# Which work stands ahead of what at the start, in the last gate groups and at the last store of a Strassen-multiplied decoder layer

## The chip, the cores and the metric

The kernel runs on one core of a Trainium2 chip. The metric is the device time of one execution in microseconds (us), as the median over several runs; lower is better. The profile is one further execution of the same program, recorded by the hardware profiler; it has a time of its own, which stands beside its span below. The core's engines are TensorE (PE in the rows, its weight loads PEld), VectorE (DVE), ScalarE (ACT), GpSimd (POOL) and SyncE (SP), which here only issues transfers.

## The reference

A decoder layer over 512 rows of width 2048 in float32. One projection makes seven blocks of 2048 columns and 16 forget logits; a causal depthwise convolution of 31 taps feeds one half of the output projection, an attention with forget gates the other; a layer norm ends it.

```python
z = einsum("bsd,de->bse", h, w_in) + b_in
glu_val, glu_gate, gate_c, q, k, v, f_logit, gate_a = split(z)
u = glu_val * sigmoid(glu_gate)
c = depthwise_causal_conv(u, w_dw, taps=31) + b_dw
y_conv = silu(layer_norm(c)) * silu(gate_c)
logits = q k^T * scale + cum[:, :, q0:q1, None] - cum[:, :, None, :q1]   # cum = cumsum(log_sigmoid(f_logit))
y_attn = softmax(causal(logits)) v * silu(gate_a)
h = layer_norm(ALPHA * h + concat(y_conv, y_attn) w_out + b_out)
```

## The kernel before

**Products.** Every float32 operand is split into a rounded part (a copy on ScalarE into fp32r, `high`, `x_high`, L797, L804) and what is left of it (a subtraction on VectorE, `low`, `x_low`, L1325, L1371). A product is three matmuls: high by high, high by low, low by high (`mm3`, L1073 to L1075). The projections follow Strassen's scheme with seven products in place of eight: x and the weights are cut into quarters, and sums of quarters of x (`X_ORDER`, factors 0 to 6) are multiplied by sums of weight blocks (`B11`, `B12`, `B22`, `SUM`, `B21`).

**Groups and slots.** There are 56 groups `g` of two weight tiles. Groups 0 to 47 (three per head: query and key, value and attention gate, convolution value and its gate) make the heads; groups 48 to 55 make the convolution's gates. `HEAD_GROUPS` is 48. A group has seven slots `s`; in a slot TensorE runs one unit of 24 matmuls (`unit(n)`), and ScalarE and VectorE make the weights of the unit two slots later (`high(n + 2)`, `low(n + 2)`). Slot 2 of a group runs the unit with m = 4 of the group before. Each engine's program is one list in a written order; an instruction that waits for a semaphore holds all behind it on its engine, and TensorE, too, takes its instructions in order.

**Sums of weight blocks.** In a group VectorE makes two sums (`sum_1`, L1336; `sum_2`, L1344), and GpSimd two with accumulating transfers (`sum_3`, L658; `sum_4`, L665). The latter gives the weights of the m = 4 unit. From group 51 on (`T4_VEC`) VectorE makes it itself (L1351).

**The start.** TensorE turns x's quarters with transposes (`turn_x`, L1139), ScalarE and VectorE round them. The forget logits have weights of their own (`f_raw`, `f_w`), rounded and multiplied beside the rest (`f_terms`, L1149 and L1151). GpSimd adds a causal mask to the rows of forget sums that SyncE has repeated over the partitions (`load_bias`, L505; `masks`, L673).

**The convolution.** A head's 31 taps are multiply-adds on VectorE (`conv`, L1432), dealt out over slots by the tables `TAPS_AT` and, for the last head, `TAPS_LAST` (a row for each group from 48 on, a number for each slot); half of a slot's taps stand ahead of its `low`, half behind. GpSimd sums the heads' results (`add_conv`, L681); when all 16 are in, one matmul with `mean_w` makes the mean (L1254), ScalarE reads it (L985), and the heads' rows are loaded back (`load_cin`, L437), centred on VectorE (`center`, L1561), squared on ScalarE (L948) and added up (`add_square`, L1568), all at the (group - 48, slot) places of `LOAD_AT`, `CENTER_AT`, `SQUARE_AT` and `ADD_AT`.

**The end.** After the groups come 112 units of the output projection and a norm. SyncE stores the rows of the output (`store_half`, L629; L635; L639).

## Time and profile before

| what | us |
|---|---|
| median of 3 runs (lowest, highest) | 1584.41 (1583.24, 1584.81) |
| the profiled execution's own time | 1583.03 |
| its span | 1581.2 |
| TensorE busy | 1552.0 (98%) |
| VectorE busy | 1445.3 (91%) |
| ScalarE busy | 840.8 (53%) |
| GpSimd busy | 248.9 (16%) |

The span runs from the first to the last instruction. A row of the timeline is: start, length, engine, line, operation, output<-input, shape, count, and in brackets how long the engine had been idle before it and what released it. Line numbers in the rows are those of the kernel before. `PEclk` is the granted TensorE clock as a share of full speed.

### The profile page before, as it was taken

Reading aid. Unit: us, or ns where it says so; the run is one execution under the profiler, and the core shown is the slowest. Engines: PE = TensorE matmul, PEld = TensorE weight load, DVE = VectorE, ACT = ScalarE, POOL = GpSimd, SP = SyncE. Lnnn points to the kernel's source line nnn. Section 1 sums busy time; section 2 is a strip of 40 time slices with the busy share of each in tenths; the row PEclk is TensorE's granted clock in tenths of the full one; section 3 lists DMA queues with packets and bytes.
Section 4 is the critical chain, followed back from the end, with each engine's and each line's share of the span. In section 5 each row is a group of like instructions: output and inputs, shape, how many; then the busy total and the mean of one; then the engine's idle time right before and its main releaser. Section 6 shows DMA issues by size and latency. Waiting matters only on the chain.

```text
span 1581.2 us, 29452 instructions
## 1 busy us (share of the span) xinstructions
PE 1552.0 (98%) x11574; PEld 1487.7 (94%) x11574; DVE 1445.3 (91%) x1975; ACT 840.8 (53%) x1225; POOL 248.9 (16%) x275
## 2 busy tenths in 40 slices
PE   7999999999999999999999999999999999999997
PEld 6999999999999999999999999999999988888885
DVE  7769999999999999999999999999989889986787
ACT  4565454554545545455454554545455576654462
POOL 1101112122121221212212122121110000000000
PEclk9999999999999999999999999999999999999998
DMA  8488889999999999999999999999899899887776
GB/s 225 113 198 190 220 203 223 220 222 233 231 228 222 222 240 224 226 219 223 236 219 233 225 221 239 224 226 218 192 275 284 238 340 343 295 238 239 267 214 192
DMA packets 316473, 365.23 MB, mean 231 GB/s; under 512 B 14561, under 2 KB 254337, under 8 KB 315025
## 3 DMA queue, kind: packets, MB, share of 16 engines
q1 hardware_dynamic: 285168, 260.45, 53.3%
q0 software_dynamic: 26784, 98.58, 34.6%
q10 hardware_dynamic: 4384, 4.33, 0.8%
q8 instruction: 92, 1.51, 0.4%
q14 instruction: 45, 0.37, 0.1%
HBM read 287.25 MB, written 87.06 MB: 237 GB/s over the span
## 4 chain that ended last, share of the span: by engine, by line
PE 85%; DVE 8%; issue 3%; DMA 2%; ACT 1%; SPq 0%; POOL 0%; DVEq 0%; ACTq 0%; POOLq 0%
PE ps L1073 28%; PE ps L1074 28%; PE ps L1075 28%; DVE whl L1325 2%; DVE c_tiles L1432 2%; PE ps L1190 1%; DVE raw L1344 1%; DMA f_raw<-in_w_in_dram 1%; DMA conv_rows_dram<-c_tiles 1%; DMA raw<-in_w_out_dram 1%; DVE xl L1371 0%; ACT whl L797 0%; PE ps L1184 0%; DVE raw L1336 0%; DMA raw<-raw 0%
## 5 line engine op out<-in xcount | busy, mean ns | idle before, releaser
L1073 PE MATMUL ps<-xh,whl 128*128 128x256 f32 x3136 | 896.1, 286 | 8.3 <-DVE whl L1325 3.7
L1074 PE MATMUL ps<-xl,whl 128*128 128x256 f32 x3136 | 888.8, 283 | 0.0
L1075 PE MATMUL ps<-xh,whl 128*128 128x256 f32 x3136 | 888.8, 283 | 0.0
L797 ACT ACTIVATE whl<-raw 128x1024 fp32r<-128x1024 f32 x392 | 415.2, 1061 | 557.9 <-PE ps L1075 472.0
L1073 PEld LDWEIGHTS ps<-xh,whl 128*128 128x128 f32 x3136 | 600.4, 191 | 11.2 <-issue 6.3
L1074 PEld LDWEIGHTS ps<-xl,whl 128*128 128x128 f32 x3136 | 600.6, 192 | 0.5 <-issue 0.5
L1075 PEld LDWEIGHTS ps<-xh,whl 128*128 128x128 f32 x3136 | 600.4, 191 | 0.0
L1325 DVE TENSOR_TENSOR whl<-raw,whl 128x1024 fp32r<-128x1024 f32 x392 | 478.7, 1221 | 56.6 <-ACT whl L797 56.5
L1432 DVE SCALAR_TENSOR_TENSOR c_tiles<-ps,taps,c_tiles 128x511 f32<-128x511 f32 (+14 forms) x480 | 350.1, 729 | 6.8
L658 POOL DMA_DIRECT2D raw<-raw x56 | 49.7, 888 | 556.4 <-DMA raw<-in_w_in_dram 446.5
L1073 PE MATMUL ps<-whl,yh 128*128 128x512 f32 x320 | 124.9, 390 | 1.2 <-issue 0.9
L1328 DVE TENSOR_TENSOR whl<-raw,whl 128x1024 fp32r<-128x1024 f32 x80 | 97.8, 1222 | 30.0 <-ACT whl L773 29.8
L1074 PE MATMUL ps<-whl,yh 128*128 128x512 f32 x320 | 124.7, 390 | 0.0
L1075 PE MATMUL ps<-whl,yl 128*128 128x512 f32 x320 | 124.6, 389 | 0.0
L773 ACT ACTIVATE whl<-raw 128x1024 fp32r<-128x1024 f32 x80 | 84.6, 1057 | 74.2 <-PE ps L1075 72.6
L665 POOL DMA_DIRECT2D raw<-raw x51 | 43.2, 848 | 310.5 <-DVE whl L1325 310.5
L1344 DVE TENSOR_TENSOR raw<-raw 128x1024 f32<-128x1024 f32 x56 | 72.7, 1299 | 1.9
L1073 PEld LDWEIGHTS ps<-whl,yh 128*128 128x128 f32 x320 | 60.1, 188 | 14.5 <-DVE whl_more L1328 1.7
L1075 PEld LDWEIGHTS ps<-whl,yl 128*128 128x128 f32 x320 | 60.1, 188 | 12.5
L1074 PEld LDWEIGHTS ps<-whl,yh 128*128 128x128 f32 x320 | 60.1, 188 | 12.4
L690 POOL DMA_DIRECT2D out_sums_dram<-in_w_out_dram x64 | 68.6, 1199 | 1.0 <-DMA out_sums_dram<-out_sums_dram 0.5
L1336 DVE TENSOR_TENSOR raw<-raw 128x1024 f32<-128x1024 f32 x56 | 68.2, 1218 | 0.0
(197 smaller groups left out, 1538.0 us busy)
## 6 DMA issues: line engine op xcount, KB each, us to landing
raw<-in_w_in_dram SPq DMA_DIRECT2D x224, 512.0 KB, 8.0
raw<-raw POOLq DMA_DIRECT2D x107, 512.0 KB, 6.0
out_sums_dram<-in_w_out_dram POOLq DMA_DIRECT2D x64, 512.0 KB, 9.6
raw<-out_sums_dram SPq DMA_DIRECT2D x64, 512.0 KB, 5.2
raw<-in_w_out_dram SPq DMA_DIRECT2D x48, 512.0 KB, 5.6
out_sums_dram<-in_w_out_dram SPq DMA_DIRECT2D x32, 512.0 KB, 9.5
out_sums_dram<-out_sums_dram SPq DMA_DIRECT2D x32, 512.0 KB, 9.4
x<-in_x_dram SPq DMA_DIRECT2D x8, 512.0 KB, 8.2
```

The costliest lines, as they stand in the source:

```text
L658: nc.gpsimd.dma_start(raw[:, ring(g, B12), :], raw[:, ring(g, B22), :], accum_op=ALU.add) \
L690: nc.gpsimd.dma_start(t_dram[t, k, :, :], src, accum_op=ALU.add).then_inc(t_added[t], 16)
L773: nc.scalar.activation(out_w(u, 0), raw_out(u), ACT.Copy).then_inc(high_done, 1)
L797: nc.scalar.activation(w_high(n), source(n), ACT.Copy).then_inc(high_done, 1)
L1073: nc.tensor.matmul(o, ah, bh, start=start, stop=False, skip_group_check=True)
L1074: nc.tensor.matmul(o, ah, bl, start=False, stop=False, skip_group_check=True)
L1075: return nc.tensor.matmul(o, al, bh, start=False, stop=True, skip_group_check=True)
L1325: vec.tensor_tensor(w_low(n), source(n), w_high(n), ALU.subtract).then_inc(low_done, 1)
L1328: vec.tensor_tensor(out_w(u, 1), raw_out(u), out_w(u, 0), ALU.subtract).then_inc(low_done, 1)
L1336: vec.tensor_tensor(raw[:, ring(g, SUM), :], raw[:, ring(g, B11), :], raw[:, ring(g, B12), :], ALU.add).then_inc(t1_done, 1)
L1344: vec.tensor_tensor(o, o, raw[:, ring(g, B22), :], ALU.add).then_inc(t2_done, 1)
L1432: vec.scalar_tensor_tensor(out=o[:, n:], in0=ps[:, U_BANK, 0:SEQ - n], scalar=tap, in1=o[:, n:], op0=ALU.mult, op1=ALU.add) \
```

## The change

The last head's taps, which stood in groups 48 to 50, stand in groups 48 to 51: group 49 has 12 in place of 15, group 50 has 10 in place of 9, and group 51 has 2. The mean matmul moves from slot 5 of group 50 to slot 2 of group 51, ScalarE's read of it from slot 6 to slot 3 of group 51, and GpSimd's addition of head 15 from group 50 to group 51. The rows of head 15 are stored by SyncE in the loads of group 52, and SyncE no longer waits for that store ahead of its other loads; the wait stands at the load of head 15 and at ScalarE's second square. Loading, centring, squaring and adding move by up to a few slots.

At the start, x's second quarter (factor 1) and the first weights are rounded ahead of the forget weights on ScalarE and VectorE, and TensorE's first unit stands ahead of the first forget terms. GpSimd's first masks stand behind `sum_4` of group 1. At the end, the first half of the first 128 output rows is stored from ScalarE's queue in place of SyncE's last place.

On ScalarE at the start, where `f_raw` and `f_w` are the forget weights, `xh` the rounded x and `whl` the rounded weights, there stood:

```order
L804 ACTIVATE xh<-ps 128x512 x4
L813 ACTIVATE f_w<-f_raw 128x16x16
L816 ACTIVATE f_w<-f_sum 128x8x16
L819 ACTIVATE f_w<-f_w 128x384
L804 ACTIVATE xh<-ps 128x512 x4
L797 ACTIVATE whl<-raw 128x1024 x2
L804 ACTIVATE xh<-ps 128x512 x4
L797 ACTIVATE whl<-raw 128x1024
```

Now there stands (the lines are those of the changed kernel):

```order
L808 ACTIVATE xh<-ps 128x512 x8
L801 ACTIVATE whl<-raw 128x1024
L819 ACTIVATE f_w<-f_raw 128x16x16
L822 ACTIVATE f_w<-f_sum 128x8x16
L801 ACTIVATE whl<-raw 128x1024
L826 ACTIVATE f_w<-f_w 128x384
L808 ACTIVATE xh<-ps 128x512 x4
L801 ACTIVATE whl<-raw 128x1024
```

The four pieces of x's second quarter and the first weights moved up past the three forget activations, and the second weights past the last of these.

On GpSimd behind the first group, where `raw` is a weight block and `probs` holds the forget sums, there stood:

```order
L658 DMA raw<-raw 128x1024
L715 TENSOR_TENSOR x<-x 128x2048
L665 DMA raw<-raw 128x1024
L658 DMA raw<-raw 128x1024
L673 TENSOR_TENSOR probs<-probs,mask 128x128 x4
L665 DMA raw<-raw 128x1024
```

Now there stands:

```order
L660 DMA raw<-raw 128x1024
L717 TENSOR_TENSOR x<-x 128x2048
L667 DMA raw<-raw 128x1024
L660 DMA raw<-raw 128x1024
L667 DMA raw<-raw 128x1024
L675 TENSOR_TENSOR probs<-probs,mask 128x128 x4
```

The masks moved behind the transfer that makes the m = 4 weights of group 1 (L665 before, L667 now); nothing else moved there.

On VectorE in slots 5 and 6 of group 49, from `sum_1` to the next weights and an eviction, where the `c_tiles` rows are taps and `th_z` is a gate, there stood:

```order
L1336 TENSOR_TENSOR raw<-raw 128x1024
L1432 SCALAR_TENSOR_TENSOR c_tiles<-ps,taps,c_tiles 128x495
L1432 SCALAR_TENSOR_TENSOR c_tiles<-ps,taps,c_tiles 128x494
L1553 SCALAR_TENSOR_TENSOR tiles<-th_z,tiles 128x512
L1432 SCALAR_TENSOR_TENSOR c_tiles<-ps,taps,c_tiles 128x493
L1325 TENSOR_TENSOR whl<-raw,whl 128x1024
L1469 TENSOR_TENSOR tiles<-nu,ps 128x256
```

Now there stands:

```order
L1345 TENSOR_TENSOR raw<-raw 128x1024
L1441 SCALAR_TENSOR_TENSOR c_tiles<-ps,taps,c_tiles 128x497
L1562 SCALAR_TENSOR_TENSOR tiles<-th_z,tiles 128x512
L1441 SCALAR_TENSOR_TENSOR c_tiles<-ps,taps,c_tiles 128x496
L1334 TENSOR_TENSOR whl<-raw,whl 128x1024
L1478 TENSOR_TENSOR tiles<-nu,ps 128x256
```

A tap's shape counts down by one column with each tap. The last tap ahead of the weights has 493 columns before and 496 now: three taps fewer have run by there, one of them in this piece and two ahead of it.

The diff, with the tables' later lines left out:

```diff
@@ -52,20 +52,20 @@
 CIN = 6
 
 
-LOAD_AT = {(3, 1): (0, 1, 2), (4, 0): (3, 4), (4, 1): (5, 6), (5, 0): (7,), (5, 1): (8, 9), (6, 0): (10, 11),
+LOAD_AT = {(3, 1): (0, 1, 2), (4, 0): (3, 4), (4, 1): (5,), (5, 0): (6,), (5, 1): (7, 8), (6, 0): (9, 10),
...
-CENTER_AT = {(3, 0): 0, (3, 3): 1, (3, 6): 2, (4, 0): 3, (4, 2): 4, (4, 3): 5, (4, 6): 6, (5, 0): 7, (5, 2): 8, (5, 3): 9,
+CENTER_AT = {(3, 4): 0, (3, 6): 1, (4, 0): 2, (4, 2): 3, (4, 3): 4, (4, 6): 5, (5, 0): 6, (5, 2): 7, (5, 3): 8, (5, 6): 9,
...
 R1, R1_ODD, R2, R5, U_BANK, BANK_A, BANK_B, BANK_C = range(8)
 
 PAIRS = ((Q, K), (V, GATE_A), (VAL, GLU))
 
 TAPS_AT = ((2, 0, 1, 2, 1, 0, 2), (2, 1, 1, 2, 3, 1, 2), (0, 1, 2, 3, 2, 1, 2))
-TAPS_LAST = ((0, 0, 0, 0, 2, 2, 3), (2, 1, 2, 2, 2, 3, 3), (2, 2, 3, 2, 0, 0, 0))
+TAPS_LAST = ((0, 0, 0, 0, 2, 2, 3), (2, 1, 1, 2, 2, 1, 3), (2, 1, 1, 2, 1, 1, 2), (2, 0, 0, 0, 0, 0, 0))
 
 PT_N = [SEQ - P * j for j in range(NT)]
 PT_AT = [0, 512, 1024, 896]
@@ -434,6 +434,8 @@
                     sp.wait_ge(cent_stored[j % CIN], 16 * (j // CIN))
                 elif j == CIN - 1:
                     sp.wait_ge(mean_var_done, 1)
+                if j == HEADS - 1:
+                    sp.wait_ge(c_stored[1], 8 * HEADS)
                 sp.dma_start(cin_slot(j), conv_dram[j, :, :]).then_inc(cin_loaded[j % CIN], 16)
 
             def loads(g):
@@ -454,6 +456,9 @@
                     sp.wait_ge(cum_stored, 16)
                     load_bias(0)
                 if g >= 1:
+                    if g == HEAD_GROUPS + 4:
+                        sp.wait_ge(conv_done, HEADS)
+                        sp.dma_start(conv_dram[HEADS - 1, :, :], c_tiles[:, 1, :]).then_inc(c_stored[1], 16)
                     for j in LOAD_AT.get((g - HEAD_GROUPS, 0), ()):
                         load_cin(j)
                     sp.wait_ge(low_done, at(g - 1, 3) + 1)
@@ -553,10 +558,8 @@
                 if g - 2 >= HEAD_GROUPS:
                     store_z2(g - 2)
                 if g == HEAD_GROUPS + 3:
-                    sp.wait_ge(conv_done, HEADS)
-                    sp.dma_start(conv_dram[HEADS - 1, :, :], c_tiles[:, 1, :]).then_inc(c_stored[1], 16)
                     sp.wait_ge(c_stored[0], 8 * HEADS)
-                    sp.wait_ge(c_stored[1], 8 * HEADS)
+                    sp.wait_ge(c_stored[1], 8 * HEADS - 16)
                     sp.wait_ge(pv_done, HEADS)
                 for j in LOAD_AT.get((g - HEAD_GROUPS, 1), ()):
                     load_cin(j)
@@ -624,7 +627,7 @@
                     if u == NORM_AT[j - 4] + 12:
                         load_z(j)
             def store_half(e, h):
-                t, c = (2, 3, 0)[e], slice(1024 * h, 1024 * (h + 1))
+                t, c = 2 + e, slice(1024 * h, 1024 * (h + 1))
                 sp.wait_ge(bpost_added, 16 * (2 * e + h + 1))
                 sp.dma_start(out[0, P * t:P * (t + 1), c], res[t][:, c]).then_inc(stored, 16)
 
@@ -637,7 +640,6 @@
                 c = slice(SEQ * n, SEQ * (n + 1))
                 sp.wait_ge(row_done, n + 2)
                 sp.dma_start(out[0, P:2 * P, c], res[1][:, c]).then_inc(stored, 16)
-            store_half(2, 0)
             sp.wait_ge(stored, 160)
 
         @block.gpsimd
@@ -713,16 +715,18 @@
                     pool.wait_ge(s3_s1_s2_done, 3)
                     pool.wait_ge(low_done, 3)
                     nc.gpsimd.tensor_tensor(x12[:, :, :], x12[:, :, :], x21[:, :, :], ALU.add).then_inc(s4_done, 1)
-                if g < HEAD_GROUPS and g % 3 == 1:
+                if 1 < g < HEAD_GROUPS and g % 3 == 1:
                     masks(g // 3)
                 if g < T4_VEC:
                     sum_4(g)
+                if g == 1:
+                    masks(0)
                 out_sums(g)
                 if g < HEAD_GROUPS and g % 3 == 0 and g >= 6:
                     add_conv(g // 3 - 2)
                 if g == HEAD_GROUPS:
                     add_conv(HEADS - 2)
-                if g == HEAD_GROUPS + 2:
+                if g == HEAD_GROUPS + 3:
                     add_conv(HEADS - 1)
 
             def repeat_row(dst, src, loaded, accum=False):
@@ -809,17 +813,17 @@
                     src = w_in[1024 * h:1024 * (h + 1), F_COL:F_COL + HEADS]
                     nc.scalar.dma_start(f_raw[:, h, :, :], src.rearrange("(k p) c -> p k c", p=P)).then_inc(f_loaded, 16)
             x_high(0)
+            x_high(1)
+            high(0)
             act.wait_ge(f_loaded, 32)
             nc.scalar.activation(f_w[:, 0:2, :, 0:HEADS].rearrange("p a k c -> p (a k) c"),
                                  f_raw[:, :, :, :].rearrange("p a k c -> p (a k) c"), ACT.Copy).then_inc(fw_high, 1)
             act.wait_ge(fw_vec, 1)
             nc.scalar.activation(f_w[:, 2, :, 0:HEADS], f_sum[:, :, :], ACT.Copy).then_inc(fw_high, 1)
+            high(1)
             act.wait_ge(fw_vec, 3)
             act.wait_ge(vec_const, 3)
             nc.scalar.activation(f_w[:, 3, :, :], f_w[:, 2, :, :], ACT.Copy, scale=-1.0).then_inc(fw_high, 1)
-            x_high(1)
-            high(0)
-            high(1)
             x_high(3)
             high(2)
             act.wait_ge(rows_turned, 1)
@@ -944,6 +948,8 @@
                 if j >= 3:
                     act.wait_ge(sq_added, j - 2)
                 nc.scalar.dma_start(conv_dram[j, :, :], cin_slot(j)).then_inc(cent_stored[j % CIN], 16)
+                if j == 1:
+                    act.wait_ge(c_stored[1], 8 * HEADS)
                 o = c_tiles[:, j % 2, :] if j else sq_sum[:, :]
                 nc.scalar.activation(o, cin_slot(j), ACT.Square).then_inc(sq_done, 1)
 
@@ -980,7 +986,7 @@
                                              ACT.Copy, scale=0.5).then_inc(taps_done, 1)
                         x_high(2)
                         forget(1)
-                    if g == HEAD_GROUPS + 2 and s == 6:
+                    if g == HEAD_GROUPS + 3 and s == 3:
                         act.wait_ge(mean_var_done, 1)
                         nc.scalar.activation(mean[:, :], ps[:, BANK_B, :], ACT.Copy).then_inc(mean_read, 1)
                     if (g - HEAD_GROUPS, s) in SQUARE_AT:
@@ -1065,6 +1071,8 @@
             deviation(2)
             scale_rows(2)
             deviation(3)
+            act.wait_ge(bpost_added, 80)
+            nc.scalar.dma_start(out[0, 0:P, 0:1024], res[0][:, 0:1024]).then_inc(stored, 16)
 
         @block.tensor
         def _(pe):
@@ -1157,9 +1165,9 @@
             for f in (0, 1):
                 for b in range(4):
                     turn_x(f, b)
-            pe.wait_ge(fw_high, 3)
+            unit(0)
+            pe.wait_ge(fw_vec, 3)
             f_terms(((0, 0, 0), (2, 0, 1)), True)
-            unit(0)
 
             def scores(i):
 
@@ -1228,6 +1236,7 @@
                     if g == 0 and s == 3:
                         f_terms(((1, 3, 1),))
                     if g == 0 and s == 5:
+                        pe.wait_ge(fw_high, 3)
                         f_terms(((3, 5, 1),)).then_inc(f_done, 1)
                         for b in range(3):
                             turn_x(2, b)
@@ -1248,7 +1257,7 @@
                         turn_p_c(g // 3 - 1)
                     if 0 < g <= HEAD_GROUPS and g % 3 == 0 and s == 4:
                         values(g // 3 - 1)
-                    if g == HEAD_GROUPS + 2 and s == 5:
+                    if g == HEAD_GROUPS + 3 and s == 2:
                         pe.wait_ge(csum_done, HEADS)
                         pe.wait_ge(ptl_done, 3 * HEADS)
                         nc.tensor.matmul(ps[:, BANK_B, :], mean_w[:, :], csum[:, :], start=True, stop=True) \
@@ -1371,8 +1380,10 @@
                         vec.tensor_tensor(lo, ps[:, x_bank(at_f + b), :], hi, ALU.subtract).then_inc(xl_done, 1)
 
             x_low(0)
+            x_low(1)
             dve.wait_ge(f_loaded, 32)
             vec.tensor_tensor(f_sum[:, :, :], f_raw[:, 0, :, :], f_raw[:, 1, :, :], ALU.add).then_inc(fw_vec, 1)
+            low(0)
             dve.wait_ge(fw_high, 2)
             dve.wait_ge(fw_vec, 1)
             vec.tensor_tensor(f_w[:, 0:2, :, LOW_AT:F_WIDE].rearrange("p a k c -> p (a k) c"),
@@ -1380,8 +1391,6 @@
                               f_w[:, 0:2, :, 0:HEADS].rearrange("p a k c -> p (a k) c"), ALU.subtract).then_inc(fw_vec, 1)
             vec.tensor_tensor(f_w[:, 2, :, LOW_AT:F_WIDE], f_sum[:, :, :], f_w[:, 2, :, 0:HEADS], ALU.subtract) \
                .then_inc(fw_vec, 1)
-            x_low(1)
-            low(0)
             for h in range(2):
                 dve.wait_ge(x_loaded["21"][h], 16)
             dve.wait_ge(xt_turned, 4)
@@ -1443,7 +1452,7 @@
                 i = g // 3 - (2 if g % 3 == 0 and s < 4 else 1)
                 if i < HEADS - 1:
                     return i, TAPS_AT[g % 3][s]
-                if g < HEAD_GROUPS + 3:
+                if g < HEAD_GROUPS + 4:
                     return HEADS - 1, TAPS_LAST[g - HEAD_GROUPS][s]
                 return 0, 0
```

## Rows read from the trace of the kernel before

**Rows 1.** TensorE's waits over the whole span: total us, times, longest.
```profile
PE ps L1073 <- DVE whl L1325: 3.7, 7, 1.5
PE ps L1073 <- DVE tiles L1473: 3.2, 3, 2.3
```

**Rows 2.** TensorE in the timeline, start.
```profile
10.45 1.09 PE L1139 MATMUL ps<-ident,x 128*128 128x128 f32 x8 [0.28 <-DMA x<-in_x_dram]
...
12.98 0.32 PE L1149 MATMUL ps<-xh,f_w 128*48 128x256 f32 x1 [1.44 <-ACT f_w L819]
...
17.13 0.38 PE L1073 MATMUL ps<-xh,whl 128*128 128x256 f32 x1 [0.20 <-DVE whl L1325]
...
20.47 0.39 PE L1073 MATMUL ps<-xh,whl 128*128 128x256 f32 x1 [0.21 <-DVE whl L1325]
...
23.45 1.91 PE L1139 MATMUL ps<-ident,xs 128*128 128x128 f32 x16
```

**Rows 3.** The load of the first weights (L427): issue, and time from issue to landing.
```profile
2.99 0.52 SPq L427 DMA_DIRECT2D raw<-in_w_in_dram  x1
...
DMA to landing us min/median/max: 9.2/9.2/9.2
```

**Rows 4.** ScalarE and VectorE in the timeline, start.
```profile
12.83 2.04 ACT L804 ACTIVATE xh<-ps 128x512 fp32r<-128x512 f32 x4
14.74 1.08 ACT L797 ACTIVATE whl<-raw 128x1024 fp32r<-128x1024 f32 x1
...
15.85 1.23 DVE L1325 TENSOR_TENSOR whl<-raw,whl 128x1024 fp32r<-128x1024 f32 x1
```

**Rows 5.** TensorE in the timeline, at its longest wait after the start.
```profile
84.58 0.58 PE L1073 MATMUL ps<-xh,whl 128*128 128x256 f32 x1 [2.26 <-DVE tiles L1473]
```

**Rows 6.** One stretch: length, busy (instructions) of PE, PEld, DVE, ACT, POOL, PEclk, DMA, GB/s.
```profile
84.50:87.90 3.40, 3.33 (x16) 3.33 (x17) 3.33 (x16) 2.50 (x7) 0.00 (x0) 0.54 0.80 218
```

**Rows 7.** VectorE and GpSimd in the timeline ahead of that wait.
```profile
64.48 1.15 DVE L1325 TENSOR_TENSOR whl<-raw,whl 128x1024 fp32r<-128x1024 f32 x1
...
75.64 1.70 POOL L673 TENSOR_TENSOR probs<-probs,mask 128x128 f32<-128x128 f32 x4 [26.62 <-DMA probs<-forget_sums_dram]
77.30 0.83 POOL L665 DMA_DIRECT2D raw<-raw  x1
```

**Rows 8.** That L665 transfer, from issue to landing.
```profile
DMA to landing us min/median/max: 4.6/4.6/4.6
```

**Rows 9.** Columns as Rows 6; a stretch, and the sum over 1100 to 1180.
```profile
1160.00:1180.00 20.00, 19.27 (x159) 18.92 (x159) 14.85 (x18) 11.11 (x16) 1.68 (x2) 1.00 1.05 313
sum 80.00, PE 75.79 PEld 73.70 DVE 73.18 ACT 36.47 POOL 12.99; mean PE 18.95 PEld 18.43 DVE 18.30 ACT 9.12 POOL 3.25
```

**Rows 10.** The page's group of the taps: busy us, mean ns, idle before.
```profile
L1432 DVE SCALAR_TENSOR_TENSOR c_tiles<-ps,taps,c_tiles 128x511 f32<-128x511 f32 (+14 forms) x480 | 350.1, 729 | 6.8
```

**Rows 11.** TensorE in the timeline, the two longest idles of groups 49 and 50.
```profile
1135.93 0.36 PE L1073 MATMUL ps<-xh,whl 128*128 128x256 f32 x1 [1.48 <-DVE whl L1325]
...
1139.80 0.39 PE L1073 MATMUL ps<-xh,whl 128*128 128x256 f32 x1 [0.76 <-DVE tiles L1473]
```

**Rows 12.** GpSimd and VectorE in the timeline, groups 50 and 51.
```profile
1150.86 2.20 POOL L681 TENSOR_TENSOR csum<-csum,c_tiles 128x512 f32<-128x512 f32 x1 [2.80 <-DVE c_tiles L1432]
1151.83 2.32 DVE L1325 TENSOR_TENSOR whl<-raw,whl 128x1024 fp32r<-128x1024 f32 x1
...
1164.00 0.69 DVE L1561 TENSOR_TENSOR cin<-cin,mean 128x512 f32<-128x512 f32 x1 [4.15 <-DMA cin<-conv_rows_dram]
```

**Rows 13.** The last row stores (L639): length ns, first and last start; their landing.
```profile
L639 SPq DMA_DIRECT2D out_dram<-res x4: 332/332/333, 1575.4 to 1577.4; - x4
...
DMA to landing us min/median/max: 2.1/2.1/2.2
```

**Rows 14.** The store behind them on SyncE's queue (L629), and its landing.
```profile
1577.79 0.46 SPq L629 DMA_DIRECT2D out_dram<-res  x1
...
DMA to landing us min/median/max: 3.0/3.0/3.0
```

More of the change, by code:

```diff
@@ L52 @@
 CIN = 6
-LOAD_AT = {(3, 1): (0, 1, 2), (4, 0): (3, 4), (4, 1): (5, 6), (5, 0): (7,), (5, 1): (8, 9), (6, 0): (10, 11),
-           (6, 1): (12, 13), (7, 0): (14, 15)}
-CENTER_AT = {(3, 0): 0, (3, 3): 1, (3, 6): 2, (4, 0): 3, (4, 2): 4, (4, 3): 5, (4, 6): 6, (5, 0): 7, (5, 2): 8, (5, 3): 9,
-             (5, 6): 10, (6, 0): 11, (6, 3): 12, (6, 6): 13, (7, 0): 14, (7, 2): 15}
-SQUARE_AT = {(3, 1): 0, (3, 4): 1, (4, 0): 2, (4, 1): 3, (4, 3): 4, (4, 4): 5, (5, 0): 6, (5, 1): 7, (5, 3): 8, (5, 4): 9,
-             (6, 0): 10, (6, 1): 11, (6, 4): 12, (7, 0): 13, (7, 1): 14, (7, 3): 15}
-ADD_AT = {(3, 6): 1, (4, 2): 2, (4, 3): 3, (4, 4): 4, (4, 6): 5, (5, 2): 6, (5, 3): 7, (5, 4): 8, (5, 6): 9, (6, 2): 10,
-          (6, 3): 11, (6, 6): 12, (7, 2): 13, (7, 3): 14, (7, 4): 15}
+LOAD_AT = {(3, 1): (0, 1, 2), (4, 0): (3, 4), (4, 1): (5,), (5, 0): (6,), (5, 1): (7, 8), (6, 0): (9, 10),
+           (6, 1): (11, 12), (7, 0): (13, 14), (7, 1): (15,)}
+CENTER_AT = {(3, 4): 0, (3, 6): 1, (4, 0): 2, (4, 2): 3, (4, 3): 4, (4, 6): 5, (5, 0): 6, (5, 2): 7, (5, 3): 8, (5, 6): 9,
+             (6, 0): 10, (6, 2): 11, (6, 3): 12, (6, 6): 13, (7, 0): 14, (7, 2): 15}
+SQUARE_AT = {(3, 5): 0, (4, 0): 1, (4, 1): 2, (4, 3): 3, (4, 4): 4, (5, 0): 5, (5, 1): 6, (5, 3): 7, (5, 4): 8, (6, 0): 9,
+             (6, 1): 10, (6, 3): 11, (6, 4): 12, (7, 0): 13, (7, 1): 14, (7, 3): 15}
+ADD_AT = {(4, 2): 1, (4, 3): 2, (4, 4): 3, (4, 6): 4, (5, 2): 5, (5, 3): 6, (5, 4): 7, (5, 6): 8, (6, 2): 9, (6, 3): 10,
+          (6, 4): 11, (6, 6): 12, (7, 2): 13, (7, 3): 14, (7, 4): 15}
 R1, R1_ODD, R2, R5, U_BANK, BANK_A, BANK_B, BANK_C = range(8)
```

## The prediction

> **What bounds the kernel now.** I read the page's busy times first (TensorE 98%, VectorE 91%), then TensorE's waits, then the timelines around each wait. Behind the start, TensorE waits in two places only, nearly always for VectorE: 3.7 us for remainders of weights and 3.2 us for evictions of results [rows 1]. One of these, 2.26 us, is in group 2 [rows 5]; nearly all others are in groups 49 to 51. Between the two places TensorE has no idle in any stretch, so a microsecond of its idle is a microsecond of time, and VectorE's load counts only where a remainder comes too late. Ahead of and behind that lie the start (transfers and rounding until products run) and the tail (norm and stores). So I price four places.
>
> **Term 1, the start: +2.0.** Before, TensorE turns the last pieces of x's second quarter from 10.45 to 11.54, idles 1.44, runs 32 forget matmuls from 12.98, a unit from 17.13, a second from 20.47, and turns the next factor from 23.45 [rows 2]. ScalarE rounds x's second quarter only at 12.83, because the forget activations stand ahead of it, and the first weights at 14.74 [rows 4]. The change lifts that block, but not the load: the first weights are issued at 2.99 and land 9.2 later, at 12.19 [rows 3]. By then ScalarE has the quarter done (the last piece is turned at 11.54, and four pieces need 2.04, overlapping the turning). From rounding to VectorE's start it takes 1.11 (14.74 to 15.85), from there to TensorE 1.28 (15.85 to 17.13) [rows 2, 4]. So the first unit starts at 12.19 + 2.39 = 14.58, 2.5 us earlier than now. But the forget matmuls, which filled TensorE from 12.98, now stand behind it. TensorE must do unit, forget terms and unit ahead of the next turning: 2.98 + 3.8 + 2.98 = 9.76 (2.98 is 23.45 - 20.47; 3.8 is 17.13 - 12.98 less the idle and the pipelined end). That ends at 24.34 against 23.45: +0.9. VectorE's two factor sums are ready sooner, and nobody is helped, since what follows (turning, ScalarE, VectorE, unit 2) hangs on that turning. The moved f_w activations and subtractions fit under the first unit; their last reader is the final forget matmul, much later.
>
> TensorE's idle grows from 1.44 to about 3.0 us (11.54 to 14.58). In group 2 an idle of 2.26 was followed by a stretch of 3.4 us with a mean granted clock of 0.54, that is 1.2 GHz for nearly all of it, in which 16 matmuls ran [rows 5, 6]. At 2.98 for 24, 16 take 1.99: a loss of 1.4. The 1.44 idle before the forget matmuls cost no clock. I add 1.1 of the 1.4, as a longer idle than 2.26 probably costs it, but not in every execution. Bounds: +0.9 (clock stays) to +2.3; a gain is excluded, since the weights can't start before 12.19.
>
> The Trainium skill (TensorE: Matmul & The Clock Gate, Part 1) says that the slow clock is the default and activity lifts it. By that rule the new gap is paid in full and this term is +2.3; without it, +0.9.
>
> **Term 2, group 2: -3.7.** GpSimd's masks wait for the repeated forget sums until 75.64, and the L665 transfer that makes the m = 4 weights of group 1 stands behind them, at 77.30, landing 4.6 later at 81.9 [rows 7, 8]. Only then do rounding, remainder and the eviction behind it run, and TensorE, ready at 82.32, starts at 84.58. What the transfer itself waits for is the remainder of m = 6, done at 65.6 (64.48 + 1.15) [rows 7]. In the new order it is issued there and lands at some 70; even at three times 4.6 it lands at 79.5, with rounding, remainder and eviction (1.1 + 1.3 + 0.4) done by 82.3. The idle goes (2.26) and so does the clock loss behind it (1.4). The masks stay where they are, held by their own data, and the next transfer of GpSimd stays behind them. What is late next: VectorE's masked maxima in slot 0 of group 2 need the masks (77.3), before the 82.3 that TensorE allows. Bounds: 2.3 (clock loss not in every run) to 3.7.
>
> **Term 3, groups 49 to 51: -3.6.** Over 1100 to 1180 TensorE is busy 75.79 of 80, so 4.2 idle [rows 9]. A tap costs 0.73 [rows 10]. A group is 7 units for TensorE, 7 x 24 x 19.27 / 159 = 20.4 us [rows 9]. The waits show VectorE too long for that in group 49, by at least the 1.48 + 0.76 that it misses [rows 11]; three taps fewer shorten it by 2.2, and group 50, with one tap more but no addition of GpSimd's beside it, stays as it is. What matters is the lead at each place. The weights that TensorE misses by 1.48 at 1135.93 have three taps fewer ahead of them: 2.2 earlier, so that idle goes with 0.7 to spare. The eviction missed by 0.76 at 1139.80 also has three fewer; TensorE arrives 1.48 earlier, and 1.48 + 0.76 - 2.19 leaves 0.05 [rows 11]. From there on, one and then two further taps are gone, and the smaller waits of group 50 (some 1.0 together) vanish. In group 51 VectorE now stands 4.15 for the first centring, since the rows are loaded late behind SyncE's wait for a store [rows 12]; the change takes that wait out and puts the centring three to four slots later, and 0.7 of idle goes with it. Remaining: 0.17 at the end of group 48, which is not touched.
>
> New in group 51: two taps, VectorE's own sum, GpSimd's addition and the mean matmul. The addition takes 2.20, and the remainder beside it 2.32 in place of 1.23 [rows 4, 12]: 1.1 more on VectorE, as now in group 50. TensorE takes its instructions in order, so a late addition would stop it: tap 31 ends some 1.2 us into slot 0 plus VectorE's lateness, the addition 2.4 later, and the matmul stands behind three units, 8.6 us. Spare is 2 us or more if VectorE is late by 3. I allow 0.3 for all that, beside the 0.2 left: 4.2 - 0.2 - 0.1 - 0.3 = 3.6. Bounds: 1.7 (VectorE still bound, below) to 4.2. The moved loads, squares and additions of squares lie under groups with VectorE busy 14.9 of 20 [rows 9]; SyncE now waits for the last tap ahead of two of the later loads only, and the load that needs the store is four groups off.
>
> The Trainium skill (SBUF — State Buffer, Who interferes with whom) has the second of two such instructions blocked until the first ends. The trace agrees (2.32). By that rule the addition's whole 2.2 could fall on the sum of group 51 rather than half of it, and this term would be 3.0.
>
> **Term 4, the tail: -1.2.** The last store on SyncE's queue is issued at 1577.79 behind four others, though its rows were ready long before, and lands at 1580.8 [rows 14]; without it the last is issued at 1577.4 and lands at 1579.5 [rows 13]. That is 1.3; I take 1.2. Bounds: 0.4 (its issue alone) to 1.3.
>
> **Sum.** 2.0 - 3.7 - 3.6 - 1.2 = -6.5. The profiled execution would go from 1583.03 to 1576.5. The median shown is 1.4 above it, so the forecast is 1584.41 - 6.5 = 1577.9. All terms at their best: -8.3, 1576.1; at their worst: 2.3 - 2.3 - 1.7 - 0.4 = -2.1, 1582.3.
>
> **Rivals.**
> - VectorE stays the bound in groups 49 and 50, since group 50 gains a tap and 12 taps still make group 49 longer than TensorE's work. For it: group 49 missed by 2.24 and gains 2.19. Against: the lead counted above, and group 50's own taps stand later than before. Term 3 gives 1.7 in place of 3.6: 1579.8.
> - The transfers are the bound behind group 50. For it: the DMA share is 1.05 over 1160 to 1180 [rows 9]. Against: nobody but GpSimd waits for a transfer of weights there. Then term 3 comes back as waits and only 2.0 - 3.7 - 1.2 = -2.9 is left: 1581.5.
> - The reordered groups hold, but the clock loss of group 2 is rare outside the profiled execution, so term 2 gives 2.3: 1579.3.
> - Slower: after the 3.0 us idle the clock falls at 14.6 and does not come back while TensorE still has gaps in group 0. A slow matmul costs 3.40 / 16 - 2.98 / 24 = 0.088 more. Break-even with 0.9 - 3.7 - 3.6 - 1.2 = -7.6 is 86 slow matmuls; if some 170 are slow, to the end of group 0, that is +15.0: 1591.8. Against: in group 2 it was back after 16, with TensorE just as busy [rows 6].
>
> **How the numbers follow.** Forecast 0.64, first rival 0.16, second 0.09, third 0.06, slow clock 0.05. What a measurement of this kernel can tell from no change is about 0.2%, 3.2 us: faster means under 1581.2. Faster: 0.64 + 0.06 + 0.14 of the first rival's 0.16 = 0.84; same: 0.02 of it and the second, 0.11; slower 0.05. The likeliest case's own range is 1576 to 1580; the range to hold 8 in 10 reaches to the second rival: 1575.5 to 1581.8.
>
> **What would show it.** Start: the first unit near 14.6, the next turning near 24.3 or, with a stretch of clock near 0.5, near 25.5. Group 2: the L667 transfer issued near 66, no idle near 82, clock 1.00 there. Groups 49 to 51: under 0.6 us of TensorE idle in all, no wait at the mean matmul, no 4 us on VectorE at the first centring. Tail: no store behind the last four, and span end some 2.1 to 2.6 behind the last one's issue. It is wrong if the next turning starts before 23.5, if TensorE waits for `csum`, or if weights are waited for from transfers behind 1160.

## The result and the profile after

| | before | changed |
|---|---|---|
| median (runs) | 1584.75 us (5, 1583.24 to 1589.20) | 1576.80 us (5, 1574.31 to 1578.41) |
| profiled execution, its span | 1583.03, 1581.2 | 1576.80, 1575.0 |
| TensorE idle over 1100 to 1180 | 4.21 | 2.16 |
| TensorE, last start to span end | 12.02 | 10.76 |

The ratio is 0.9946, with an interval of 0.9931 to 0.9961: faster by 0.5%. The forecast was 1577.9. The profiled executions differ by 6.2 us (forecast 6.5). I split that by the start of the same VectorE instruction in both traces (the remainders of weights, 504 in each). Behind the start the changed kernel is 2.15 late. Behind group 2 it is 1.70 early, a step of -3.86. Behind group 51 it is 4.92 early, a step of -3.22, and the tail gives 1.2 more.

**Start.** TensorE and ScalarE of the changed kernel in the timeline (columns as in [rows 2]), and the stretch behind the first of them (columns as in [rows 6]):

```profile
14.81 0.58 PE L1081 MATMUL ps<-xh,whl 128*128 128x256 f32 x1 [2.96 <-DVE whl L1334]
...
25.61 1.15 PE L1147 MATMUL ps<-ident,xs 128*128 128x128 f32 x9
```
```profile
12.43 1.06 ACT L801 ACTIVATE whl<-raw 128x1024 fp32r<-128x1024 f32 x1
```
```profile
14.60:18.40 3.80, 3.59 (x19) 3.59 (x20) 3.48 (x5) 1.47 (x2) 0.00 (x0) 0.58 1.10 350
```

The next turning stands at 25.61, against 23.45 [rows 2]. The first matmul behind 2.96 us of idle lasts 0.58 and the granted clock is 0.58 over the stretch, so TensorE ran at its slow level of 1.2 GHz for most of it.

**Group 2.** GpSimd in the timeline, then a stretch of all engines:

```profile
68.08 0.86 POOL L667 DMA_DIRECT2D raw<-raw  x1 [16.91 <-DVE whl L1334]
78.54 2.24 POOL L675 TENSOR_TENSOR probs<-probs,mask 128x128 f32<-128x128 f32 x4 [9.61 <-DMA probs<-forget_sums_dram]
```
```profile
80.00:90.00 10.00, 10.00 (x86) 10.00 (x85) 6.51 (x18) 8.28 (x17) 2.33 (x4) 1.00 0.87 211
```

The transfer now stands ahead of the masks (before: behind them, at 77.30 [rows 7]), TensorE has no idle, and its clock is 1.00.

**Groups 49 to 51.** TensorE's remaining waits, and the two instructions of ScalarE that stand ahead of the last of them:

```profile
1115.17 0.39 PE L1081 MATMUL ps<-xh,whl 128*128 128x256 f32 x1 [0.17 <-DVE tiles L1482]
...
1136.39 0.39 PE L1081 MATMUL ps<-xh,whl 128*128 128x256 f32 x1 [0.77 <-DVE tiles L1482]
...
1146.51 0.39 PE L1081 MATMUL ps<-xh,whl 128*128 128x256 f32 x1 [1.22 <-ACT p L867]
```
```profile
1145.04 1.06 ACT L801 ACTIVATE whl<-raw 128x1024 fp32r<-128x1024 f32 x1 [3.27 <-DMA raw<-raw]
1146.00 0.46 ACT L867 ACTIVATE p<-ps,cols 128x256 f32<-128x256 f32 x1
```

The 1.48 [rows 11] and the small waits are gone. The eviction that TensorE missed by 0.76 is missed by 0.77 still. And there is a wait of a new kind: ScalarE stands 3.27 us for a weight sum's transfer, and an eviction that TensorE needs is queued behind it. More rows bear on these waits: a remainder of VectorE with an idle of 0.47 ahead of it, and GpSimd's queue, where two other transfers (`out_sums_dram`) are issued ahead of the sum's (L660):

```profile
1119.28 1.23 DVE L1334 TENSOR_TENSOR whl<-raw,whl 128x1024 fp32r<-128x1024 f32 x1 [0.47 <-ACT whl L801]
```
```profile
1121.35 2.00 POOL L692 DMA_DIRECT2D out_sums_dram<-in_w_out_dram  x2
...
1136.61 0.88 POOL L660 DMA_DIRECT2D raw<-raw  x1 [13.26 <-DMA raw<-in_w_in_dram]
```

GpSimd's addition of head 15, which waits for the last tap, stands in group 51, with VectorE's own sum beside it. TensorE does not wait at the mean matmul:

```profile
1157.22 2.20 POOL L683 TENSOR_TENSOR csum<-csum,c_tiles 128x512 f32<-128x512 f32 x1 [2.08 <-DVE c_tiles L1441]
1158.30 2.20 DVE L1353 TENSOR_TENSOR raw<-raw 128x1024 f32<-128x1024 f32 x1
```

**Tail.** SyncE's last rows: four stores and nothing behind them. They land 2.1 us after their issue, as before [rows 13].

```profile
1570.45 2.32 SPq L642 DMA_DIRECT2D out_dram<-res  x4
```

### The profile page after: what moved, and what is told of

Read it like the earlier page. It is cut to its first block, busy times and chain, and to the rows that moved or that the text cites. A ratio compares the mean times of both kernels' runs of the same rounds, so it can differ in the third digit from the quotient of the medians.

```text
span 1575.0 us, 29453 instructions
## 1 busy us (share of the span) xinstructions
PE 1550.6 (98%) x11574; PEld 1488.1 (94%) x11574; DVE 1445.4 (92%) x1975; ACT 841.7 (53%) x1225; POOL 248.2 (16%) x275
## 4 chain that ended last, share of the span: by engine, by line
PE 91%; DVE 6%; issue 1%; DMA 1%; ACT 1%; SPq 0%; DVEq 0%; ACTq 0%
PE ps L1081 29%; PE ps L1082 29%; PE ps L1083 29%; DVE whl L1334 2%; DVE c_tiles L1441 1%; PE ps L1198 1%; PE ps L1147 1%; DVE raw L1353 1%; DMA raw<-in_w_out_dram 1%; PE ps L1192 0%; ACT whl L801 0%; DMA x<-in_x_dram 0%; DVE xl L1380 0%; DVE raw L1345 0%; PE ps L1157 0%
## 5 line engine op out<-in xcount | busy, mean ns | idle before, releaser
L660 POOL DMA_DIRECT2D raw<-raw x56 | 49.4, 882 | 558.1 <-DMA raw<-in_w_in_dram 452.9
L667 POOL DMA_DIRECT2D raw<-raw x51 | 43.2, 848 | 319.9 <-DVE whl L1334 319.9
```

The lines of the kernel that those rows point to most:

```text
L660: nc.gpsimd.dma_start(raw[:, ring(g, B12), :], raw[:, ring(g, B22), :], accum_op=ALU.add) \
```

## The experiments

Times of one kernel differ by some us between executions, so an edit is read from its profile, stage by stage, and by its median only where there are many runs. Each profile is one execution. "Behind the start" and the like are differences of the same VectorE instruction's start, against the kernel before unless said otherwise.

### One part alone, or all but one

**e1, only the start** (the kernel before, with the changed order on ScalarE, VectorE and TensorE up to the second unit):

```
 x_high(0)
+x_high(1)
+high(0)
 act.wait_ge(f_loaded, 32)
```

> The kernel before with the new order at the start alone (ScalarE, VectorE and TensorE), nothing else. Theory A (TensorE's work in series): the first unit starts near 14.8 us, the forget terms and the second unit behind it, and the next turning near 25.6 us, 2.1 later than before's 23.45: 0.9 of work that stood in the old gap and 1.2 of half clock. The shift stays to the end: about +2.1 us, 1586.5. Rival B (what the rounding was moved for): the earlier first unit brings everything forward by up to 2.3 us: 1582. Rival C: the shift is eaten by the wait in group 2, whose masks come from the forget sums at an own time: 0.

Median 1590.15 (12 runs) against 1585.50 for before (17); ratio 1.0018, interval 1.0002 to 1.0033. Behind the start it is 2.4 late, behind group 2 and at group 50 2.5. So nothing of the start's loss is taken back later. Group 2 came out the same by another way: TensorE idled 2.44 at 87.13, its clock stayed at 1.00, and waits for remainders (one of 0.50) followed in place of the slow stretch of [rows 6].

The medians differ by 4.65, more than the start's part. The profiled execution loses 5.3 us in groups 50 and 51, which the changed start does not explain. TensorE, GpSimd, and the stretch behind it:

```profile
1159.55 2.08 PE L1255 MATMUL ps<-csum,mean_w 128*128 128x512 f32 x2 [4.02 <-POOL csum L681]
```
```profile
1153.32 6.17 POOL L681 TENSOR_TENSOR csum<-csum,c_tiles 128x512 f32<-128x512 f32 x1 [2.80 <-DVE c_tiles L1433]
```
```profile
1158.00:1166.00 8.00, 6.45 (x27) 5.42 (x28) 0.71 (x2) 0.60 (x1) 2.39 (x2) 0.57 0.84 227
```

GpSimd's addition took 6.17 us where it takes 2.20 in the kernel before [rows 12]; TensorE waited 4.02 for it, and the granted clock of the stretch was 0.57. VectorE beside it was not held up: it ran two remainders in 2.35, where the second of them alone took 2.32 before [rows 12].

```profile
1153.16 2.35 DVE L1326 TENSOR_TENSOR whl<-raw,whl 128x1024 fp32r<-128x1024 f32 x2
```

**e2, all but the masks' place:**

```
-    if g == 1:
-        masks(0)
-if 1 < g < HEAD_GROUPS and g % 3 == 1:
+if g < HEAD_GROUPS and g % 3 == 1:
```

> The changed kernel with GpSimd's first masks back ahead of the transfer that makes the m = 4 weights of group 1. Theory A: the idle of 2.3 us in group 2 and the half clock behind it come back, and remainders of weights from group 3 on stand 3.9 us later than in the changed kernel; the wait shifts with the start (near 86.7 us). Rival B: with the start 2.1 later the wait is shorter, since it hangs on transfers and not on TensorE: less than 2 us.

1580.06 (one run). Group 2 is as before: 2.50 us of idle at 85.42 and a clock of 0.56 behind it, where the changed kernel has neither:

```profile
85.42 0.58 PE L1079 MATMUL ps<-xh,whl 128*128 128x256 f32 x1 [2.50 <-DVE tiles L1480]
```
```profile
14.60:18.40 3.80, 3.80 (x32) 3.72 (x33) 3.29 (x4) 1.47 (x2) 0.00 (x0) 1.00 1.10 350
84.00:88.00 4.00, 2.58 (x12) 2.58 (x13) 3.97 (x16) 3.08 (x6) 0.00 (x0) 0.62 0.60 146
```

From behind the start to behind group 2 it loses 0.2 against before, where the changed kernel gains 3.86. But here the clock did not fall at the start, behind 3.13 us of idle, and the next turning stood at 24.06: the start cost 0.6 and no more. Of nine profiles with this start (the changed kernel twice, e1 to e4, e7 to e9) it is the only one.

**e3, all but the taps** (tables, taps, addition and mean matmul as before):

```
-    if g == HEAD_GROUPS + 3:
+    if g == HEAD_GROUPS + 2:
         add_conv(HEADS - 1)
```

> The changed kernel with the last head's taps, the mean, its read, the store of head 15 and the four tables as before. Theory A: TensorE's idle over groups 49 to 51 goes from 2.2 back to 4.2 us and six waits, each of which costs some 0.2 to 0.3 more than its idle row shows, since the matmuls behind it start late by a refill: 3.2 us in all. Rival B: only the idle counts: 2.0 us. From the start to group 48 nothing moves against the changed kernel.

1580.17 (one run), 3.4 above the changed kernel. All waits of before are back (1.49, 0.77, 0.40, 0.65, 0.60, 0.51), and over groups 49 to 51 it loses 0.4 against before where the changed kernel gains 3.22. So that gain is the taps' and not the masks':

```profile
1134.28 0.36 PE L1076 MATMUL ps<-xh,whl 128*128 128x256 f32 x1 [1.49 <-DVE whl L1329]
...
1138.15 0.39 PE L1076 MATMUL ps<-xh,whl 128*128 128x256 f32 x1 [0.77 <-DVE tiles L1477]
```

**e4, all but the last store:**

```
+store_half(2, 0)
 sp.wait_ge(stored, 160)
```

> The changed kernel with the first half of the first 128 output rows stored last on SyncE's queue again. Theory A: that store is issued behind the four others and lands 3.0 us after: +1.2 us from TensorE's last matmul to the span's end, all else the same. Rival B: only its issue time counts: +0.4.

1580.86 (one run). From TensorE's last start to the end 12.02 against 10.76: 1.26 for the store. The rest of the 4.1 is not the tail's. It lies near 540 us, where this execution loses 3.2 and the changed kernel's does not. A load issued at 521 landed 19.1 us later in place of 13.4, and ScalarE waited 7.17 us for it. In e5 the same load landed after 18.6.

### The start

**e5, the start in its old order, all else changed** (e1's lines taken back).

> The changed kernel with its start in the old order (forget matmuls ahead of the first unit, old order on ScalarE and VectorE). My account: the start alone costs 2.15 us of profiled time against before, 0.9 of it TensorE work in series and 1.2 half clock behind the 2.96 us of idle. Then here the forget matmuls start near 13.0, the next turning near 23.45, the clock stays at 1.00 over 14 to 18, and the span is 2.15 shorter than the changed kernel's 1575.0: about 1572.9; median about 1574.6. Rival 1: the order of the start is of no use or cost outside the profiled execution (the first weights' load varies more than that): same median as the changed kernel, 1576.8. Rival 2: the old start leaves a later piece late (second unit or the quarter's low part), so that less than 1 us comes back: 1575.8.

Median 1575.41 (4 runs, 1574.58 to 1576.97), with the kernel before at 1588.43 (7) beside it; ratio 0.9914 (0.9891 to 0.9937). Behind the start it is 2.12 earlier than the changed kernel. Its profiled execution then lost 4.0 near 540 us, and it had no wait for ScalarE at 1145. So its span (1575.2) tells nothing of the edit.

**e6, the gap filled:**

```
+for n in range(18):
+    nc.tensor.transpose(ps[:, U_BANK, 0:P], ident[:, :], ident[:, :])
 unit(0)
```

> The changed kernel with 18 turnings of the identity (128x128, results unused) on TensorE between the first turnings and the first unit, into a bank that the unit overwrites: TensorE is then busy for some 1.5 to 2.5 us of the 2.96 us gap. If the half clock behind the gap comes from the idle, the granted clock is 1.00 over 14.6 to 18.4, the first unit still starts near 14.6 and the next turning stands near 24.4 in place of 25.6; span about 1.2 below the changed kernel. Rival: the clock falls for another reason (time since the start), then 0.58 stands there again and the next turning stays at 25.6; or the turnings run past 14.8 and push the first unit by as much as they save.

TensorE's rows and the stretch that answers to the changed kernel's 0.58:

```profile
11.61 2.13 PE L1169 MATMUL ps<-ident 128*128 128x128 f32 x18
14.84 0.39 PE L1081 MATMUL ps<-xh,whl 128*128 128x256 f32 x1 [1.10 <-DVE whl L1336]
24.32 1.91 PE L1147 MATMUL ps<-ident,xs 128*128 128x128 f32 x16
```
```profile
14.60:18.40 3.80, 3.56 (x30) 3.50 (x31) 3.44 (x5) 1.47 (x2) 0.00 (x0) 1.00 1.10 352
```

The first unit starts where it did (14.84), the clock is 1.00, and the next turning comes 1.29 earlier. So the half clock cost 1.29 in the changed kernel's profile, and 24.32 - 23.45 = 0.87 is what the order costs without it. That the idle is what drops the clock rests on more than this one profile: the four with an idle of at most 1.6 us here (before, e5, e6, e10) have 1.00, and eight of the nine with 2.9 to 3.2 have 0.50 to 0.66. The run took 1574.21 (one), its span is 2.6 below the changed kernel's. Only half of that is the start's; 1.1 lies in groups 49 to 51, where this execution had no wait for ScalarE either.

### Groups 49 to 51

**e7, GpSimd's two accumulating transfers of group 49 behind the weight sum of group 50:**

```
-out_sums(g)
+if g != HEAD_GROUPS + 1:
+    out_sums(g)
...
 sum_3(g)
+if g == HEAD_GROUPS + 2:
+    out_sums(HEAD_GROUPS + 1)
```

> The changed kernel with GpSimd's two accumulating transfers of group 49 (out sums) issued behind its weight sum of group 50 in place of ahead of it. My account: they run beside the load of B's weights of group 50 (issued near 1123.6, landing 12.5 later), which makes that load, then the sum transfer (1136.6, landing 8.4), then ScalarE's rounding (3.27 us of wait) and the eviction behind it late, and TensorE waits 1.22 us at 1146.5. Moved away, the load lands in 9 to 10, ScalarE waits under 1 us and TensorE's 1.22 is gone with its restart: groups 49 to 51 shorter by 1.3 to 1.5, span near 1573.6 if the start is as in the changed kernel. Rival: what sets the load's landing is all the queues' traffic there (DMA share near 1), then it still lands in 12 and the 1.22 stays; or the two accumulates now delay the next sum on GpSimd's queue and a wait of 0.5 to 1 us appears behind 1150.

1578.35 (one run). The load issued at 1124.5 landed after 4.2 us, where it takes 12.1 to 12.6 in every other profile. The sum's transfer was issued 6 us earlier, and ScalarE's 3.27 and TensorE's 1.22 are gone. So the two transfers are what makes the load and the sum late. (The wait alone would not show it, since e5 and e6 have none without this edit.) But the transfers now meet the next loads, one of which landed 15.9 us after issue, and ScalarE waits for it:

```profile
1154.02 2.95 ACT L804 ACTIVATE whl<-raw 128x1024 fp32r<-128x1024 f32 x3 [6.25 <-DMA raw<-in_w_in_dram]
```
```profile
1156.48 0.36 PE L1084 MATMUL ps<-xh,whl 128*128 128x256 f32 x1 [1.60 <-DVE whl L1337]
```

Against the changed kernel groups 49 to 51 are 0.6 longer. The start cost more here than in any other profile, 3.1 us: behind an idle of 2.99 the slow clock lasted longer, and the next turning stood at 26.59 (columns as in [rows 6]).

```profile
14.60:18.40 3.80, 3.80 (x18) 3.80 (x19) 3.35 (x4) 1.47 (x2) 0.00 (x0) 0.50 1.10 352
18.40:22.00 3.60, 3.60 (x25) 3.29 (x24) 2.95 (x3) 0.00 (x0) 0.00 (x0) 0.72 1.17 285
```

**e8, the taps placed otherwise:**

```
-TAPS_LAST = (..., (2, 1, 1, 2, 2, 1, 3), (2, 1, 1, 2, 1, 1, 2), (2, 0, 0, 0, 0, 0, 0))
+TAPS_LAST = (..., (2, 1, 1, 2, 2, 1, 2), (1, 1, 2, 2, 1, 1, 2), (2, 1, 0, 0, 0, 0, 0))
```

> The changed kernel with the taps of the last four groups placed otherwise (group 49: 2 1 1 2 2 1 2 over its seven slots, group 50: 1 1 2 2 1 1 2, group 51: 2 1 0 0 0 0 0), the counts by group nearly as they are. My account of the 0.77 us that TensorE waits for an eviction at 1136.4: in slot 2 of group 49 VectorE has no tap to fill the time from its sum to ScalarE's rounded weights (0.47 of wait), so it comes 0.47 later to all that follows. With a tap there and one less elsewhere that 0.47 and with it most of the 0.77 goes: 0.5 to 1.0 shorter, the 1.22 at 1146.5 stays (it waits for a transfer). Rival: VectorE's total load is what is late, so the 0.77 stays wherever the taps are; or the emptied slot stalls in its turn and nothing changes in sum.

1577.32 (one run). The edit leaves slot 2 of group 49 as it was, with one tap, so it does not test what its expectation says of VectorE's 0.47 there, and the 0.47 is still there (at 1119.30). The 0.77 is gone: one tap of 0.73 fewer in the last slot of group 49 is enough. But tap 31, a slot later, makes the addition and the mean matmul late, as neither account had it, and groups 49 to 51 are 0.7 longer than in the changed kernel:

```profile
1161.65 1.12 PE L1263 MATMUL ps<-csum,mean_w 128*128 128x512 f32 x2 [1.41 <-POOL csum L683]
```

**e9, one tap moved** from the end of group 49 to group 50, tap 31 left where it is: `(2, 1, 1, 2, 2, 1, 2), (2, 1, 2, 2, 1, 1, 2), (2, 0, 0, 0, 0, 0, 0)`.

> The changed kernel with one tap moved from the last slot of group 49 to the third slot of group 50 (12 and 10 taps become 11 and 11, group 51 keeps its 2). My account: VectorE is late at the end of group 49 only; one tap less ahead of the last eviction takes the 0.77 us of TensorE's wait at 1136.4 and its restart (0.28) away, and since the last tap stays where it is, GpSimd's addition is not late as it was when tap 31 slipped a slot: 1.0 shorter over groups 49 to 51, no wait at the mean matmul, if the wait of 0 to 1.2 us for ScalarE's weights at 1145 to 1147 comes out as in the changed kernel. Rival: the 1.0 comes back inside group 50 as a wait for an eviction or a remainder, since VectorE has one tap more there: 0.3 shorter or nothing.

1575.28 (one run). The 0.77 is gone and nothing waits for the addition:

```profile
1145.23 0.38 PE L1081 MATMUL ps<-xh,whl 128*128 128x256 f32 x1 [0.87 <-ACT p L867]
```

Groups 49 to 51 are 1.14 shorter. The wait for ScalarE is 0.87, with a sum that landed in 7.6 us, not 8.4, so not all of the 1.14 need be the tap's.

**e10, both edits that helped (e5 and e9), and e11, the changed kernel beside it:**

> The changed kernel with its start in the old order and the one tap moved. The two add up if my account holds: -2.1 at the start, -1.0 in group 49: a profiled span near 1571.9, median near 1573.5 and below both kernels, ratio to the changed kernel 0.998. Rival 1: the two share a wait for transfers behind 1140 that takes the second gain: 1574.8. Rival 2: the start's gain is taken by late transfers elsewhere (a load near 540 us that landed 18.6 us after its issue instead of 13.4 made TensorE wait in two runs): then medians of 1575 to 1577 with much scatter.

> The changed kernel, unaltered, beside the kernel of both edits on the same chip: median 1576.8 as before. If the half clock behind the 2.96 us of idle at the start is not in every execution, this profile may show a clock of 1.00 over 14.6 to 18.4 and a next turning near 24.4; my account gives the half clock again. The wait at 1145 to 1147 for ScalarE's weights comes between 0 and 1.3 us, by how long the weight sum's transfer takes (under 7.7 none, 8.4 cost 1.22).

e10: median 1575.62 (6 runs, 1573.84 to 1578.33), ratio to before 0.9941 (0.9925 to 0.9957). e11: 1578.21 (6 runs, 1574.72 to 1580.50), ratio 0.9953 (0.9938 to 0.9968); before beside them 1584.34 (11). By the two ratios e10 is ahead of the changed kernel by 0.1%, within their intervals; by the medians it is ahead by 2.6 and by the profiled spans (1572.5 and 1575.4) by 2.9. Against e11's profile it is 2.35 earlier behind the start and 3.2 behind group 51. So the tap gave 0.85 here: with the 0.77 gone, TensorE comes earlier to the wait behind it.

```profile
1143.73 0.39 PE L1081 MATMUL ps<-xh,whl 128*128 128x256 f32 x1 [1.49 <-ACT p L867]
```

In e11 that wait is 1.55 and in e5 none, with sums that landed in 8.6 and 6.6 us. It goes with a transfer that varies from one execution to the next.

## Why the prediction was right, step by step

**Start: forecast +2.0, measured +2.15.** The mechanism was right. The 0.9 of work in series is 0.87 (e6 against before), but two small misses cancel in it. The work from the first unit to the next turning took 9.48 (24.32 - 14.84) and not 9.76, since work that follows without a wait takes less: 2.87 and not 2.98 for a unit, 3.63 and not 3.8 for the forget matmuls. And the first unit started at 14.84 and not at 14.58. In e2, where it started at 14.56, the order cost 0.6. The clock's part was put at 1.1 of a possible 1.4 and is 1.29 (e6 against the changed kernel). That it does not come in every execution was right too (e2). The upper bound of 2.3 was too low: e1 is 2.4 late and e7 3.1. The rival of a clock that stays low to the end of group 0 did not come; e7's clock was back behind 22 us.

The Trainium skill (TensorE: Matmul & The Clock Gate, Part 1) has the slow clock as the default. By that rule the start would cost 2.3: seven of the nine profiles are 2.0 to 2.4 late, e7 is 3.1 late, and e2, with 0.6, does not fit.

**Group 2: forecast -3.7, measured -3.86.** Idle 2.26 and the clock behind it both went, and both came back in e2. Nothing waited for the masks, which run until 80.8 now. The sum of the two is shown, its split is not: in e1 the clock stayed at 1.00 behind an idle of 2.44, and group 2 was not shorter for it, since TensorE waited for remainders in its place.

**Groups 49 to 51: forecast -3.6, measured -3.22,** and here the number is near by luck: two steps failed, and a third thing that I had left out made up for them. I left at most 0.6 of idle; 2.16 is there.

The first failed step is "1.48 + 0.76 - 2.19 leaves 0.05". I counted three taps fewer ahead of the eviction and took VectorE to be busy all the time. With less to do it ran into ScalarE, whose rounding it needs, and stood 0.47 at 1119.28. So the eviction came 1.72 earlier against group 48 (1139.34 and 1135.92, less 1.70) and not 2.19. TensorE, for its part, arrived 1.72 earlier and not 1.48, since a wait costs more than its idle (below). The two together are the 0.7 by which the 0.05 was wrong. This is worked out from the rows and not isolated: no run filled the 0.47.

The second failed step is "nobody but GpSimd waits for a transfer of weights there". ScalarE waits for the sum's transfer, 3.27 us; before, the sum landed at 1145.70 and ScalarE rounded it at 1145.92 with no idle ahead. My second rival named it (transfers as the bound), with all of the gain lost; it took 1.22 and its restart.

What offset them is the price of a wait. In the timeline the start before the 0.77 wait is at 1135.34 and the one behind it at 1136.39: 1.05 where two starts in a row are 0.12 apart, and the next is 0.23 away. So a wait of 0.77 costs 1.04, and one of 1.48 costs 1.71: about 0.25 beside the idle for each restart behind a wait. TensorE's idle fell by 4.21 - 2.16 = 2.05, but seven waits (as e3 lists them, with a 0.16) became three, and four restarts make most of the rest of 3.22.

How near the sum comes also hangs on the execution. Six profiles have the changed kernel's taps and its transfers:

| profile | step of groups 49 to 51 | TensorE's wait for ScalarE | sum's landing |
|---|---|---|---|
| changed | -3.2 | 1.22 | 8.4 |
| e2 | -2.8 | 1.65 | 8.9 |
| e4 | -3.5 | 0.96 | 8.5 |
| e5 | -4.7 | none | 6.6 |
| e6 | -4.3 | none | 7.7 |
| e11 | -2.9 | 1.55 | 8.6 |

Without the second failed step the gain is 4.3 to 4.7, above the bound of 4.2 that I had set, which counted idle alone.

**The addition in group 51: right.** It took 2.20, and VectorE's sum beside it 2.20, where the others of these groups take 1.23: no wait at the matmul, with spare. e8 shows how little: one slot more and TensorE waits 1.41.

**Tail: forecast -1.2, measured -1.2,** and 1.26 by e4.

Of the rivals, none came whole. VectorE was no longer the bound of group 50 (its waits went). The clock loss in group 2 is in two of the three profiles that idle there (before and e2, not e1).

## What to carry to other kernels

Where an engine that was late is relieved, count the waits for others that were hidden by its lateness: here the two waits that stayed hold half of the idle that should have gone. An idle of TensorE costs more than its row. Each restart adds a quarter of a microsecond, and a fallen clock added 1.3 to 1.5 us at the start in seven profiles and 2.6 in e7 (from the first unit to the next turning, against e6's 9.48). Cheap work that fills the idle kept the clock at 1.00 in the one profile that tried it (e6). A transfer moved out of one crowded place (e7) can be late in the next one. And where a step hangs on a transfer, one profile of it is not enough: read it in several.

## What the runs showed of the hardware that I had not expected

- The same idle does not always drop the clock: 3.13 us did not in e2 (1.00), 2.96 did in the changed kernel (0.58). In group 2, 2.26 did in the kernel before [rows 5, 6] and 2.50 in e2, and 2.44 did not in e1.
- GpSimd's addition took 1.26 where it began with VectorE idle (e8, its last one; the remainder that began 0.41 behind it took 1.94), 2.2 in all others of the 13 profiles but one, and 6.17 in e1. In e1 and before, the last addition began 0.16 to 0.17 behind a remainder of VectorE (1153.32 and 1153.16; 1150.86 and 1150.69). Before, the next remainder was held up (2.32). In e1 no VectorE instruction was held up, and the addition ended only at 1159.49, so it seems to have stood back behind several of them. The Trainium skill (SBUF — State Buffer, Who interferes with whom) has the second blocked until the first ends; e1 shows a wait that lasts longer than one instruction. In e1 that cost some 5 us with the clock. Whether it spreads the runs of before (up to 1593.73 beside e1, where no run of the changed kernel is above 1580.5), and so adds to the gain that the medians show, was not measured.
- The same load, issued near 521 us, landed 11.7 us (e8) to 19.1 us (e4) after its issue over the 13 profiles. Up to 16.5 (e6) TensorE did not wait for it; at 18.6 (e5) and 19.1 (e4) the executions lost 4.0 and 3.2 us there.
